# Layer 0's expert gather with eight fetch buffers in place of twelve

## The chip, the cores and the metric

The kernel runs on one core of a Trainium2 chip. The metric is the time of one execution on the device in microseconds (us). Two runs of the kernel before took 4397.53 and 4405.12 us, median 4401.32.

## The reference

The reference computes two layers of a diffusion backbone over 512 latent and 256 context tokens of width 1024, in f32. Layer 0 mixes tokens by a Fourier transform and a bidirectional state-space scan, layer 1 by latent attention. After each mixer comes the same channel mixer, PEER, which is what this change touches:

```python
q = (hb @ p["peer_wq"]).reshape(PEER_TOKEN_BLOCK, PEER_HEADS, 2, PEER_QDIM // 2)
s = jnp.einsum("thsd,hskd->thsk", q, p["peer_keys"]).astype(jnp.float32)
s_top, i_top = lax.top_k(s, PEER_TOPK)
...
u = jnp.take(p["peer_u"], experts, axis=0)
act = jax.nn.gelu(jnp.einsum("thkd,td->thk", u, hb)...) * gates
v = jnp.take(p["peer_v"], experts, axis=0)
return jnp.einsum("thk,thkd->td", act.astype(v.dtype), v)
```

Each token picks 16 of 16384 experts in each of 8 heads. An expert is a row u and a row v of 1024 numbers. The token's dot product with u, through a gelu and times a gate, is the weight with which v is added to the token's output. Layer 0 does this for all 768 tokens, layer 1 for the 512 latent ones.

## The kernel before

The whole core memory is one tensor, the arena, and all places in it are given by hand as offsets. `peer_block` runs the channel mixer for a layer. It works on tiles of 128 tokens, one token on each partition, six tiles in layer 0 and four in layer 1. A *step* is one head of one tile (48 in layer 0). A step has 16 *gathers*: gather k fetches, for each of the 128 tokens, the row pair (u, v) of its k-th expert, 2048 f32 numbers a token, 1 MB in all, into one buffer. Four gathers make a *position* (`BATCH`), so layer 0 has 192 positions and 768 gathers. Both rows of an expert stand side by side in HBM, so one indirect DMA fetches both.

The order of work is written out by hand, engine by engine, with semaphores between the engines:

- GpSimd (lines 1663 to 1680) only issues the gathers. Before each step it waits for the step's expert numbers, and before each gather it waits until the buffer's earlier gather has been used (semaphore `free`). The buffer of a gather comes from `slot_of` (line 1447): the gathers go round the buffers of the map in order.
- VectorE (`dot_batch`, line 2198) waits for each landing and computes the dot product of u with the token's row, line 2206. After the dots of a position it does other work in a fixed order: `choose_a` or `choose_b`, the two halves of a later step's choice of experts (line `half_at`, 1421: one half per position, until all 48 steps are chosen, at position 92), and the gated identity for the next two positions (line 2194).
- ScalarE (`diagonals`, line 2036) applies the gelu (line 2040) and writes four scaled diagonal matrices (line 2046).
- TensorE multiplies each diagonal with v and adds into the tile's output (line 1876), eight products for a position; the second product of each gather raises `free`. Between positions TensorE also computes queries (line 1764) and scores for later choices (`query_at`, one event for up to four tiles), and, from position 130 on, the down projection of layer 1's attention for finished tiles (`prepare`, line 1800).
- At the change of a tile VectorE gates the tile's output and adds it to x (`add_tile`, lines 2212 and 2214), and TensorE's first products of the next tile wait for that.
- The queue of SyncE loads query weights and keys for the coming events, then the weights of the down projection, and at the end of the gather the query and key weights of the attention (lines 1654 to 1661). The last two go where the first fetch buffers lie, so they wait until buffers 0 to 2, and 0 to 4, have been used for the last time.

Layer 1 has its own map with twelve buffers, of which the first 16 gathers use only eight; it is not changed. The core of GpSimd's loop is

```python
if uses:
    pool.wait_ge(free["sem"], at(free, prev + 1))
...
pool.indirect_dma_start(slots[n], None, tbl,
                        bass.IndirectOffsetOnAxis(ap=expert[:, ring[c], k:k + 1], axis=0)
                        ).then_inc(land[n]["sem"], up(land[n], 16))
```

Of the kernel before, what the change touches and what calls it, by code (L numbers as in the profile page):

```python
# [53 lines left out]
RO = XO + TT * D  # L54
SLOT = 4096
HO = RO + 3 * SLOT
L0 = HO + KD * TOK
# [1169 lines left out]
def attention_stage(core, d):  # L1227
# [30 lines left out]
    with nc.Block() as block:  # L1258
# [94 lines left out]
ROWS = 2 * D  # L1353
# [10 lines left out]
               [(7, (2, 3, 4, 5)), (0, (1,)), (0, (2, 3, 4, 5)), (1, (1,))] +  # L1364
               [(h, (2, 3, 4, 5)) for h in range(1, PH - 1)],
     "heads": (ALL, ALL[2:] + ALL[:2]) + (ALL[7:] + ALL[:7],) * 4, "kept": (), "order": None, "w": RO,
     "choose_from": 1, "spread_at": (1, 2), "small": 12, "ring_from": 0,
     "g1": L0 + 15360, "g2": L0 + 17408,
     "diag": L0 + 18432, "wq": L0 + 19968, "sc": L0 + 22016, "keys": L0 + 24064,
     "rep": (L0 + 3072, L0 + 5120), "ht": HO,  # L1370
     "slots": [RO + n * ROWS for n in range(6)] + [L0] + [L0 + 7168 + n * ROWS for n in range(5)]},
    {"events": [(h, (0,)) for h in range(4)] + [(h, (0, 1, 2, 3)) for h in range(4, PH)] +
               [(h, (1, 2, 3)) for h in range(4)],
     "heads": (ALL,) + (ALL[4:] + ALL[:4],) * 3, "kept": (4, 5, 6, 7),
# [1076 lines left out]
```

## Time and profile before

| | |
|---|---|
| median of two runs | 4401.32 us |
| profiled execution | 4394.9 us from first to last instruction (its span) |
| layer 0's gather | from 721.7 us (first issue) to 2707.1 us (last dot) |
| busy in the whole span | TensorE 3112.4 us (71%), VectorE 2859.6 (65%), GpSimd 1584.1 (36%), ScalarE 1122.0 (26%) |
| software DMA queue (the gathers) | 1342.26 MB, 73.8% of sixteen engines' span |
| mean granted clock of TensorE | 0.843 |

Times in the profile count from the first instruction. PE is TensorE, DVE is VectorE, ACT is ScalarE, POOL is GpSimd, SP is SyncE. A row of a timeline gives the start, the duration, the engine, the line, the operation, how many are merged into the row, and in brackets how long the engine sat idle before it and what ended that. "DMA to landing" is the time from the start of the issue to the last of the sixteen engines' signals.

### The profile page before, as it was taken

What the parts mean: (1) busy time and instruction counts of PE and PEld (TensorE: products, weight loads), DVE (VectorE), ACT (ScalarE), POOL (GpSimd) and SP (SyncE); (2) the same over time, 40 slices, a digit from 0 to 9 for tenths busy, and PEclk for the clock granted to TensorE, in tenths of its full rate; (3) what the DMA queues carried; (4) which work ended last, traced back from release to release, by engine and by line L of the source; (5) the groups of instructions that cost most, each with busy time, mean ns of one, the idle gap of its engine ahead of it and who ended that gap; (6) DMA issues with size and microseconds to landing.
All of it is one profiled execution on the core that took longest, in us unless ns stands there. A gap on an engine that the chain in (4) does not pass through costs nothing. (4 is left out here: it accounts for less than half of the span.)

```text
span 4394.9 us, 37634 instructions
## 1 busy us (share of the span) xinstructions
PE 3112.4 (71%) x12112; PEld 1324.7 (30%) x12112; DVE 2859.6 (65%) x7084; ACT 1122.0 (26%) x2966; POOL 1584.1 (36%) x1383
## 2 busy tenths in 40 slices
PE   7999987676666865656666656999876755555555
PEld 4655554332222321111222112565432311111111
DVE  2524853988888897555555555665788898555554
ACT  1122531322232322111222211563332222111111
POOL 0002401545444454444444441001344455444443
PEclk9999998888887887777787887999987877777777
DMA  4114734999999999999999996103999999999998
GB/s 172 39 39 146 264 105 170 408 420 421 420 420 409 402 421 420 421 421 417 412 415 421 415 421 286 39 1 116 403 420 420 419 421 417 418 420 418 418 420 340
DMA packets 223656, 1471.78 MB, mean 335 GB/s; under 512 B 25436, under 2 KB 29244, under 8 KB 53220
## 3 DMA queue, kind: packets, MB, share of 16 engines
q0 software_dynamic: 184320, 1342.26, 73.8%
q1 hardware_dynamic: 37764, 123.17, 7.8%
q10 hardware_dynamic: 1376, 3.96, 0.2%
q8 instruction: 96, 1.57, 0.1%
q14 instruction: 100, 0.82, 0.0%
HBM read 1467.02 MB, written 2.28 MB: 334 GB/s over the span
## 5 line engine op out<-in xcount | busy, mean ns | idle before, releaser
L1876 PE MATMUL banks<-arena 128*64 128x512 f32 x5120 | 1672.8, 814 | 1215.1 <-ACT arena L2046 1172.1
L1678 POOL DMA_INDIRECT arena<-experts,arena x1280 | 1507.7, 1178 | 2300.9 <-PE banks L1876 1478.7
L2206 DVE CUSTOM_DVE_ANT_0 arena<-arena 128x1024 f32<-128x1024 f32 x1280 | 1535.0, 1224 | 788.7 <-DMA arena<-experts,arena 788.5
L1876 PEld LDWEIGHTS banks<-arena 128*64 128x64 f32 x5120 | 458.4, 185 | 2356.0 <-ACT arena L2046 1364.7
L2040 ACT ACTIVATE arena<-arena 128x4 f32<-128x4 f32 x320 | 66.1, 206 | 2339.7 <-DVE arena L2206 2339.6
L2046 ACT ACTIVATE arena<-arena 128x64 f32<-128x64 f32 x1280 | 340.6, 336 | 36.3
L1764 PE MATMUL banks<-arena 128*128 128x512 f32 (+3 forms) x960 | 288.5, 455 | 6.0 <-DMA arena<-wq 5.4
L434 PE MATMUL banks<-arena 128*128 128x512 f32 (+1 forms) x640 | 208.6, 486 | 1.9 <-PEq L201 1.9
L1764 PEld LDWEIGHTS banks<-arena 128*128 128x128 f32 x960 | 160.6, 191 | 112.0 <-issue 86.6
L870 POOL TENSOR_TENSOR arena<-arena 128x256 f32<-128x256 f32 x48 | 41.2, 858 | 423.6 <-POOLq L625 332.3
L1697 PE MATMUL banks<-arena 128*128 128x512 f32 x416 | 185.4, 599 | 2.3 <-PEq L953 1.5
L434 PEld LDWEIGHTS banks<-arena 128*128 128x128 f32 x640 | 120.6, 190 | 86.2 <-issue 78.6
L2040 ACT ACT_TABLE_LOAD x90 | 115.5, 1283 | 1.6
L2194 DVE TENSOR_TENSOR arena<-arena 128x512 f32<-128x512 f32 x160 | 109.5, 685 | 0.0
L2206 DVE DVE_READ_ACCUMULATOR2_ANT arena<- 128x1 f32 x1280 | 105.9, 83 | 0.0
L1697 PEld LDWEIGHTS banks<-arena 128*128 128x128 f32 x416 | 77.6, 192 | 92.5 <-issue 92.4
L1962 ACT ACT_TABLE_LOAD x80 | 102.6, 1283 | 1.4
L1308 DVE TENSOR_REDUCE arena<-banks 128x1 f32<-128x768 f32 x64 | 61.2, 956 | 58.8 <-PE banks L1271 56.6
L1271 PE MATMUL banks<-arena 96*128 96x512 f32 (+1 forms) x256 | 96.5, 501 | 1.9 <-PEq L1600 1.5
L455 PE MATMUL banks<-arena 128*128 128x512 f32 x192 | 83.2, 593 | 0.0
L777 ACT ACTIVATE arena<-banks,arena 128x128 f32<-128x128 f32 x192 | 54.8, 368 | 105.9 <-PE banks L888 105.8
L1096 PE MATMUL banks<-arena 128*128 128x512 f32 (+1 forms) x192 | 75.4, 540 | 0.0
(250 smaller groups left out, 2942.7 us busy)
## 6 DMA issues: line engine op xcount, KB each, us to landing
arena<-l_w_ada SPq DMA_DIRECT2D x48, 1024.0 KB, 5.0
arena<-wq SPq DMA_DIRECT2D x54, 512.0 KB, 7.9
arena<-experts,arena POOLq DMA_INDIRECT x1280, 17.1
arena<-l_w_in SPq DMA_DIRECT2D x7, 2048.0 KB, 7.9
arena<-l_w_out SPq DMA_DIRECT2D x4, 1536.0 KB, 8.8
arena<-l_w_o SPq DMA_DIRECT2D x4, 1024.0 KB, 10.0
arena<-keys SPq DMA_DIRECT2D x27, 128.0 KB, 10.4
arena<-gates SPq DMA_DIRECT2D x6, 512.0 KB, 6.5
```

The costliest lines, as they stand in the source:

```text
L434: i = pe.matmul(o[:, a:b], wt[:, k, (u % 4) * P:(u % 4 + 1) * P], ht[:, k, a:b], start=(k == 0), stop=(k == KD - 1))
L455: i = pe.matmul(core["ps"][:, n % 4, :], ht[:, k, t * P:(t + 1) * P], wt[:, k, :], start=(k == 0), stop=(k == KD - 1))
L1271: i = pe.matmul(o[:, a:b], qt[0:QK, h, q * P:(q + 1) * P], kt[0:QK, h, a:b], start=True, stop=True)
L1678: pool.indirect_dma_start(slots[n], None, tbl, bass.IndirectOffsetOnAxis(ap=expert[:, ring[c], k:k + 1], axis=0)).then_inc(land[n]["sem"], ...
L1697: i = pe.matmul(core["ps"][:, bank_of(c), :], lhs(k, t), wcols[c][:, k, :], start=(k == 0), stop=(k == K - 1))
L1764: i = pe.matmul(core["ps"][:, 2 + side, 0:len(g) * P], wq[:, side, k, :], ht[:, k, g[0] * P:(g[-1] + 1) * P], start=(k == 0), stop=(k == K ...
L1876: mm = pe.matmul(core["ps"][QS * j:QS * j + QS, c, :], diag[:, g % 2, k, :], v[:, D + c * 512:D + (c + 1) * 512], start=(g % (NB * PH) == ...
L1962: act.activation(raised, shifted, ACT.Exp, accum_out=total[:, 0:1]).then_inc(exd["sem"], up(exd))
L2040: act.activation(gel[:, s], dots[:, s], ACT.Gelu).then_inc(gl["sem"], up(gl))
L2046: ins = act.activation(diag[:, g % 2, j, :], gated[:, b // 2, b % 2 * BATCH + j, :], ACT.Copy, scale=gel[:, b * BATCH + j:b * BATCH + j + 1])
L2194: dve.tensor_tensor(gated[:, n % 2], ident2.unsqueeze(1).to_broadcast([P, TOPK // 2, QS]), bcast(gate[:, ring[c], n % 2 * 8:n % 2 * 8 + 8] ...
L2206: dve.tensor_tensor_reduce(u, u, rep[i // PH % 2][:, k % NQ, :], 1.0, 0.0, ALU.mult, ALU.add, dots[:, k:k + 1]).then_inc(dot["sem"], up(dot))
```

## The change

Layer 0's map gets eight buffers. `small` goes from 12 to 8, and the list of places keeps its first eight entries; the last four are gone. Everything else follows from the length of that list: `slot_of`, the semaphores for the landings, and the gather that each wait names.

```diff
-     "choose_from": 1, "spread_at": (1, 2), "small": 12, "ring_from": 0,
+     "choose_from": 1, "spread_at": (1, 2), "small": 8, "ring_from": 0,
...
-     "slots": [RO + n * ROWS for n in range(6)] + [L0] + [L0 + 7168 + n * ROWS for n in range(5)]},
+     "slots": [RO + n * ROWS for n in range(6)] + [L0, L0 + 7168]},
```

The four places that fall out are used by nothing else.

## Rows read from the trace of the kernel before

**Rows 1.** The page: what the DMA moved, in 40 slices of the span.

```profile
GB/s 172 39 39 146 264 105 170 408 420 421 420 420 409 402 421 420 421 421 417 412 415 421 415 421 286 39 1 116 403 420 420 419 421 417 418 420 418 418 420 340
```

**Rows 2.** Busy windows: length, PE, PEld, DVE, ACT, POOL, clock, DMA share, GB/s.

```profile
761.00:1708.00 947.00, 636.46 (x2624) 250.10 (x2624) 841.10 (x2517) 274.24 (x697) 468.25 (x364) 0.83 1.01 415
1708.00:2708.00 1000.00, 600.95 (x1942) 187.50 (x1942) 545.25 (x930) 183.37 (x605) 426.41 (x389) 0.78 1.00 415
```

**Rows 3.** Waits: line 2206 in 761 to 1708, all in 1708 to 2708.

```profile
  DMA arena<-experts,arena: 29.4, 32
...
DVE arena L2206 <- DMA arena<-experts,arena: 421.5, 353, 2.3
```

**Rows 4.** Timeline of VectorE's dots, second half.

```profile
1797.04 1.23 DVE L2206 CUSTOM_DVE_ANT_0 arena<-arena 128x1024 f32<-128x1024 f32 x1 [1.25 <-DMA arena<-experts,arena]
1806.98 1.23 DVE L2206 CUSTOM_DVE_ANT_0 arena<-arena 128x1024 f32<-128x1024 f32 x1 [1.25 <-DMA arena<-experts,arena]
1819.41 1.23 DVE L2206 CUSTOM_DVE_ANT_0 arena<-arena 128x1024 f32<-128x1024 f32 x1 [0.64 <-DMA arena<-experts,arena]
```

**Rows 5.** Timeline of TensorE and GpSimd in the same stretch.

```profile
1809.69 5.79 PE L1876 MATMUL banks<-arena 128*64 128x512 f32 x16 [4.60 <-ACT arena L2046]
1813.64 0.94 POOL L1678 DMA_INDIRECT arena<-experts,arena  x1 [4.62 <-PE banks L1876]
```

**Rows 6.** Timeline of last dots and of one gather issue, first half.

```profile
1144.46 1.22 DVE L2206 CUSTOM_DVE_ANT_0 arena<-arena 128x1024 f32<-128x1024 f32 x1
1153.44 1.23 DVE L2206 CUSTOM_DVE_ANT_0 arena<-arena 128x1024 f32<-128x1024 f32 x1
1164.36 1.22 DVE L2206 CUSTOM_DVE_ANT_0 arena<-arena 128x1024 f32<-128x1024 f32 x1
1174.28 1.23 DVE L2206 CUSTOM_DVE_ANT_0 arena<-arena 128x1024 f32<-128x1024 f32 x1 [0.95 <-DMA arena<-experts,arena]
1151.11 1.98 POOL L1678 DMA_INDIRECT arena<-experts,arena  x1 [4.51 <-PE banks L1876]
```

**Rows 7.** Landings: second half; issues at 721.7; 768.8; 3051.4 (eight); 3099.5.

```profile
DMA to landing us min/median/max: 11.7/17.3/26.6
...
DMA to landing us min/median/max: 6.4/6.4/6.4
...
DMA to landing us min/median/max: 6.6/6.6/6.6
...
L1678 POOL DMA_INDIRECT arena<-experts,arena x8: 934/940/1651, 3051.4 to 3061.0; - x8
...
DMA to landing us min/median/max: 5.5/11.5/17.8
...
DMA to landing us min/median/max: 5.7/5.7/5.7
```

**Rows 8.** Timeline of a wide query event, TensorE and GpSimd.

```profile
1173.76 7.03 PE L1764 MATMUL banks<-arena 128*128 128x512 f32 x16
1180.72 3.65 PE L1876 MATMUL banks<-arena 128*64 128x512 f32 x16
1183.43 1.51 POOL L1678 DMA_INDIRECT arena<-experts,arena  x1 [5.87 <-PE banks L1876]
```

**Rows 9.** Timeline of a down projection, VectorE, TensorE and GpSimd.

```profile
2256.05 1.23 DVE L2206 CUSTOM_DVE_ANT_0 arena<-arena 128x1024 f32<-128x1024 f32 x1 [1.25 <-DMA arena<-experts,arena]
2255.13 9.31 PE L1800 MATMUL banks<-arena 128*128 128x512 f32 x32
2266.57 1.85 POOL L1678 DMA_INDIRECT arena<-experts,arena  x1 [8.48 <-PE banks L1876]
```

**Rows 10.** Waits, second half; SP's last load; its landing by the DMA view.

```profile
PE banks L1876 <- DVE arena L2214: 15.6, 3, 5.8
...
2707.57 0.49 SPq L1660 DMA_DIRECT2D arena<-l_w_ukv  x1
...
arena<-l_w_ukv SPq DMA_DIRECT2D x1, 2048.0 KB, 14.1
```

## The prediction

> **What bounds the kernel now.** I read the page's 40 slices first, then the busy windows of layer 0's gather, then who waits for whom in it, and last single positions in time. The gather runs from slice 7 to slice 24, and from slice 7 to 23 the DMA moves 402 to 421 GB/s [rows 1]. The two windows of it say the same: the DMA share is full in both, while VectorE is busy 841 of 947 us in the first and 545 of 1000 us in the second [rows 2]. The kernel has 192 positions of four gathers in this layer; half a choice of experts follows the dots of each of the first 93, which is what fills VectorE until 1708 us. So the second half is bound by the DMA alone: VectorE idles before its dots until a fetch lands, 421.5 us in 353 pieces [rows 3]. In the first half that wait is 29.4 us [rows 3], because VectorE and the DMA need nearly the same time: the last dots of three successive positions start at 1144.46, 1153.44 and 1164.36, intervals of 8.98 and 10.92, together 19.90 [rows 6]. The DMA's own pace, from two last dots that both waited for a landing, is 1806.98 - 1797.04 = 9.94 per position, 2.49 per gather [rows 4], so 19.9 for two positions. Both resources are full there, so a hole in the stream of transfers isn't filled again later.
>
> **What the change removes.** No instruction goes and none is added: 768 gathers, their dots, diagonals and products stay. GpSimd's wait before a gather now names the product that read the buffer eight gathers ago instead of twelve, so a position's fetch waits for the position two before it, not three. GpSimd does nothing else in the gather, so only fetches are queued behind that wait. With twelve buffers, the time from the release to the need was three positions less the processing; with eight it is two. That is the whole sum: does one turn of a buffer fit into two positions, 19.9 us?
>
> **The turn, second half.** Let T be the start of a position's last dot. At T = 1806.98 gelu and diagonals follow, the products start at 1809.69, and the first gather that reuses a freed buffer is issued at 1813.64, T + 6.66 [rows 4, 5]. Under the change this issue fetches for the position two later, whose first dot starts at 1819.41 [rows 4] and can't be later without a loss, since the DMA feeds it without pause. It has 1819.41 - 1813.64 = 5.77 us to land. How long does a fetch take that has little queued ahead? The median of 17.3 us [rows 7] is 6.9 gathers' worth of pace, mostly queueing, and says nothing here. The nearest rows are fetches that found the DMA empty or nearly so: 6.4, 6.6, 5.5 and 5.7 us [rows 7]; the mean is 6.05, and I take 6.1. The first of them had cold queues and the second still had two fetches ahead of it, so 5.5 is the lower end and 6.6 the upper. At 6.1 the turn is 6.66 + 6.1 + 3 x 2.49 = 20.2, 0.3 over two positions. Both positions of a pair are late by the same amount at once, so I charge a pair once: 0.3, plus 0.1 as an estimate for the step starts, where GpSimd takes one more wait first. 1708 to 2708 us holds 50 pairs: 50 x 0.4 = **20 us** (ends: 0 at 5.5; 50 x 0.9 = 45 at 6.6).
>
> **The turn, first half.** At T = 1144.46 the issue is at 1151.11, T + 6.65 [rows 6]. Here the position two later finishes its dots at 1164.36, and its first fetch must have landed 7.46 before, at 1156.90: 5.8 us to land, the same as above. But VectorE's intervals alternate, 8.98 and 10.92, and the DMA needs 9.94 for each; that fits only if the even position is in place about 1.0 ahead of its last dot, and this lead must now come out of the turn. With P for two positions, the lead is P less the turn L, and the rest has to hold 9.94 + 10.92, so P = (9.94 + 10.92 + L) / 2. With L = 6.65 + 6.1 + 7.46 = 20.2, P = 20.53, 0.63 more than 19.90. 46 pairs lie between 761 and 1708: **29 us** (ends: L = 19.6 gives 0.33, so 15; L = 20.7 gives 0.88, so 40).
>
> **Disturbances that twelve buffers absorb.** A third position in flight covers a late release; two don't. Eight wide query events fall into the first half. In one of them TensorE runs a query of 7.03 us from 1173.76, the position's products start only at 1180.72, and the issue is at 1183.43, which is 9.15 after that position's T of 1174.28, 2.5 more than the usual 6.65 [rows 6, 8]. 8 x 2.5 = **20 us** (ends: 16, where part lands beside the DMA's own load of the weights; 40, if each event's two positions both cost). Five times in the second half the down projection of the next layer's preparation takes TensorE 9.31 us; at T = 2256.05 the issue comes at 2266.57, T + 10.5, 3.9 over the usual [rows 9]. 5 x 3.9 = **20 us** (ends 10 and 30). At five changes of tile TensorE waits for VectorE's add; three such waits of the second half come to 15.6 us with one of 5.8 in it [rows 10]. The longest, less the 4.60 that TensorE idles before its products in any position [rows 5], is 1.2, so I take one microsecond each: **5 us** (0 to 10).
>
> **Start and end.** The first pass issues eight fetches at once instead of twelve; the four others were needed only after VectorE's work of the start. I take 0; if that cover is missing it costs at most one position's transfer, 10 us. At the end the load of the key weights waits for buffer 4, which is now last used in the last position rather than the one before, some six microseconds later. Before, it was issued at 2707.57 behind the query weights and took 14.1 us to land [rows 10]; issued later it finds those gone, so its landing stays, cost 0 (at most 3). Layer 1 has its own ring and doesn't change.
>
> Sum: 20 + 29 + 20 + 20 + 5 = 94 us. The profiled execution took 4394.9 us, 6.4 below the median of 4401.3; I put the sum on the median: **4495 us**. The lower ends sum to 41 (4442), the upper ones to 165 and 13 for start and end (4579).
>
> On the latency a page of the Trainium skill speaks, "DMA: Bandwidth & Descriptors", section "Anatomy of one DMA — SWDGE (gpsimd) path": a GpSimd-issued DMA takes about 2.0 us plus its bytes at 436 GB/s, which for the 1 MB of a gather gives an estimate of 4.4 us. The trace's shortest landing here is 5.5 us [rows 7], so it doesn't agree at either end. By that rule the turn would be 18.5 and both turn terms would vanish.
>
> **Rivals.** *Two positions cover the turn (not slower).* A fetch behind one or two others lands as soon as the one ahead of it plus 2.49, and the bare latency stays at or under 5.5 us; then the turn is 19.6, under 19.9, and only part of the disturbances is left: 41 us or less, around 4440, within 2%. The place is the first fetch of each position, the price up to 53 us less than forecast, and it decides where the landing takes less than 5.8 us. For it: the landings of 5.5 and 5.7 [rows 7], and the 6.6 may have been queueing only. Against it: the cold 6.4, and disturbances that have no slack left even at 5.5. That page's rule is this rival's mechanism. Chance 0.28, with the cases in between.
>
> *The latency grows in the stream (much slower).* The queue runs nearly dry each time, and the slowest of the sixteen engines ends the landing, say 7.8 us after the issue instead of 6.1. Then the second half's turn is 21.9, 2.0 over (100 us), and the first half's L of 21.9 exceeds the formula's P, so it costs 2.0 x 46 = 92; with the 45 of disturbances and some overlap of the two, 4401 + 237 = about 4640. For it: in the burst of eight issued from 3051.4 to 3061.0 the longest landing was 17.8 us [rows 7], where 5.5 and seven transfers of 2.49, less the 9.6 between first and last issue, give 13.3; other loads may be in that. Against it: the stream holds 2.49 exactly where it is fed [rows 4]. Chance 0.18.
>
> *The change doesn't do what it says.* The list of places and the small ring both have eight entries, so the ring has eight; a gain could come only from weights queueing behind fewer fetches, and VectorE and DMA would stay full. Chance 0.02, 4395.
>
> The forecast has 0.52. The range goes to 4438 below, where the pure disturbance case begins, and to 4610 above, past the upper ends and part way to the third case. About 2% (88 us) is what a measurement of this kernel tells from no change; that line, 4489, runs just below my forecast. Of the span from 4442 to 4579, 0.66 lies above it, so slower has 0.52 x 0.66 + 0.18 = 0.52, within 2% 0.46, and faster keeps the 0.02 of the last rival.
>
> **What would show it.** GpSimd's issue to landing falls from 17.3 us to about 7 to 9. The second half grows from 1000 to about 1043 us, DVE's wait for landings grows by as much, and the DMA's rate falls from 415 to about 400 GB/s. In the first half DVE's wait for landings, 29.4 us, rises above 60. If the rate stays at 415, the turn fits and I am too high; if single last dots stand more than 10.6 apart all through the second half, the latency is over 7 and I am too low. A change in layer 1 or in the attention would contradict the whole account.

## The result and the profile after

The changed kernel takes 4599.11 us (two runs, 4597.70 and 4600.52) where the kernel before takes 4401.32 us: 1.0449 times as long, with a 95% interval of 1.0433 to 1.0466. I had forecast 4495 us, so the direction was right, and the size, 198 us, is twice the 94 us of my sum. The profiled execution has a span of 4598.5 us against 4394.9.

The page's row of the DMA's rate in 40 slices answers to [rows 1]:

```profile
GB/s 165 55 21 185 267 38 242 380 384 375 389 382 366 388 372 384 380 381 378 389 370 367 379 382 378 140 37 22 273 418 419 421 416 418 421 421 419 419 421 340
```

From slice 7 to slice 24 the gather of layer 0 now gets 366 to 389 GB/s where it had 402 to 421; it is some 9% slower everywhere in this layer, in both halves. From slice 29 to slice 38, in layer 1, which has its own ring, the rate is back at 416 to 421. So the loss is a slower flow, not a few stalls.

Busy windows of the changed kernel, with the columns of [rows 2]: the 947 us of the first half, and the second half from its start to the last dot.

```profile
761.00:1708.00 947.00, 620.52 (x2464) 243.24 (x2464) 771.02 (x2291) 251.69 (x641) 417.87 (x330) 0.79 0.95 376
1799.00:2905.00 1106.00, 619.49 (x1942) 191.60 (x1942) 547.41 (x929) 183.48 (x605) 429.96 (x392) 0.75 0.96 378
```

The second half holds nearly the same work as the second window of [rows 2] (VectorE 547 against 545 us) and takes 1106 us instead of 1000. The DMA share fell only from 1.00 to 0.96 while the rate fell by 9%: so the share understates a starved stream, and the GB/s column is the one to read. The granted clock of TensorE fell too, from 0.78 to 0.75 in the second half and from 0.83 to 0.79 in the first. It has no part in the loss: the release, into which TensorE's products go, comes as soon after the dots as before (below).

Who waited for landings in those two windows, answering to [rows 3]:

```profile
  DMA arena<-experts,arena: 105.4, 94
```

```profile
  DMA arena<-experts,arena: 528.8, 370
```

29.4 us became 105.4 in the first window, which now ends some nine positions short of the work that it held before (up to 1799 us, where the first half now ends, it is 112.9), and 421.5 became 528.8 in the second, 107.3 more. The last dots of the positions, counted from 0, give the same division: from the one of position 1 to the one of position 92 the gather took 946.0 us before and 1038.2 now, +92.2; from there to the end 999.4 and 1106.1, +106.7. Together that is 199 of the 203.6 us by which the span grew. Five more lie behind the gather: 0.4 between its last dot and layer 1's first gather, 4.4 in layer 1's gather (1329.8 before, 1334.2 now). The 4.4 don't belong to the change: the two kernels below with twelve places and a wait of eight, which lose the same in layer 0, have 1329.9 and 1328.7 there.

Where in a position is the time lost? The timeline of some of VectorE's dots in a quiet stretch of the second half (compare [rows 4]; the last dots of four positions start at 1932.09, 1941.99, 1953.45 and 1963.96):

```profile
1932.09 1.22 DVE L2206 CUSTOM_DVE_ANT_0 arena<-arena 128x1024 f32<-128x1024 f32 x1 [1.25 <-DMA arena<-experts,arena]
...
1941.99 1.23 DVE L2206 CUSTOM_DVE_ANT_0 arena<-arena 128x1024 f32<-128x1024 f32 x1 [1.21 <-DMA arena<-experts,arena]
...
1944.48 1.22 DVE L2206 CUSTOM_DVE_ANT_0 arena<-arena 128x1024 f32<-128x1024 f32 x1 [0.62 <-DMA arena<-experts,arena]
...
1948.48 1.23 DVE L2206 CUSTOM_DVE_ANT_0 arena<-arena 128x1024 f32<-128x1024 f32 x1 [2.77 <-DMA arena<-experts,arena]
...
1950.98 1.23 DVE L2206 CUSTOM_DVE_ANT_0 arena<-arena 128x1024 f32<-128x1024 f32 x1 [1.26 <-DMA arena<-experts,arena]
...
1953.45 1.23 DVE L2206 CUSTOM_DVE_ANT_0 arena<-arena 128x1024 f32<-128x1024 f32 x1 [1.23 <-DMA arena<-experts,arena]
...
1956.24 1.23 DVE L2206 CUSTOM_DVE_ANT_0 arena<-arena 128x1024 f32<-128x1024 f32 x1 [1.56 <-DMA arena<-experts,arena]
...
1963.96 1.23 DVE L2206 CUSTOM_DVE_ANT_0 arena<-arena 128x1024 f32<-128x1024 f32 x1 [1.45 <-DMA arena<-experts,arena]
...
1968.81 1.23 DVE L2206 CUSTOM_DVE_ANT_0 arena<-arena 128x1024 f32<-128x1024 f32 x1 [3.01 <-DMA arena<-experts,arena]
```

And GpSimd's first issues of three positions in the same stretch, answering to [rows 5]:

```profile
1938.74 0.94 POOL L1678 DMA_INDIRECT arena<-experts,arena  x1 [7.09 <-PE banks L1876]
...
1948.64 1.88 POOL L1678 DMA_INDIRECT arena<-experts,arena  x1 [4.57 <-PE banks L1876]
...
1960.62 0.94 POOL L1678 DMA_INDIRECT arena<-experts,arena  x1 [6.35 <-PE banks L1876]
```

T = 1932.09 gives an issue at 1938.74, T + 6.65, and 1941.99 gives 1948.64, T + 6.65: the release is the one of the kernel before (the third, 1960.62, comes at T + 7.17). What it fetches is wanted by the first dots at 1944.48, 1956.24 and 1968.81. These dots start 5.74, 7.60 and 8.19 us after the issues. Where one is as short as 5.74, the dot is on time but the next one comes 4.00 us later instead of 2.49 (1944.48 to 1948.48). The last dots stand 9.90, 11.46 and 10.51 us apart. The time from an issue to the last dot of its position is what counts, and in no position of this gather is it below the 13.6 us that I had (6.1 and three times 2.49; the shortest is 13.76): 1938.74 to 1953.45 is 14.71, 1948.64 to 1963.96 is 15.32.

Over positions 94 to 129, a quiet stretch, it is 15.31 us in the median and 15.48 in the mean, of which 7.80 and 7.87 to the first dot. 6.65 + 15.48 = 22.1 is the turn; two positions take 22.1 us there, before 20.0. That the two agree is no proof: from a last dot to the issue, and from there to the last dot two positions on, is the same path measured in two pieces. What the pieces tell is which of them grew. The first half has the same turn with VectorE's work around it (compare [rows 6]):

```profile
1164.33 1.23 DVE L2206 CUSTOM_DVE_ANT_0 arena<-arena 128x1024 f32<-128x1024 f32 x1 [0.54 <-DMA arena<-experts,arena]
...
1174.24 1.23 DVE L2206 CUSTOM_DVE_ANT_0 arena<-arena 128x1024 f32<-128x1024 f32 x1 [0.94 <-DMA arena<-experts,arena]
...
1186.01 1.23 DVE L2206 CUSTOM_DVE_ANT_0 arena<-arena 128x1024 f32<-128x1024 f32 x1 [0.77 <-DMA arena<-experts,arena]
```

```profile
1170.98 1.98 POOL L1678 DMA_INDIRECT arena<-experts,arena  x1 [7.53 <-PE banks L1876]
```

1164.33 + 6.65 = 1170.98, and from there 15.03 to 1186.01: two positions in 21.68 us, 1.8 more than the 19.90 of [rows 6].

Last, the SyncE queue's load of the key weights, to be held against [rows 10]:

```profile
arena<-l_w_ukv SPq DMA_DIRECT2D x1, 2048.0 KB, 9.0
```

It is issued 6.4 us after the last dot and lands in 9.0 us instead of 14.1, and layer 1's first gather comes 344.7 us after the last dot, before 344.3.

### The profile page after: what moved, and what is told of

Same layout as the page of the kernel before. It is cut to its first block and busy times, and to the rows that moved or that the text cites. A ratio compares the mean times of both kernels' runs of the same rounds, so it can differ in the third digit from the quotient of the medians.

```text
span 4598.5 us, 37630 instructions
## 1 busy us (share of the span) xinstructions
PE 3163.0 (69%) x12112; PEld 1335.0 (29%) x12112; DVE 2869.1 (62%) x7084; ACT 1121.3 (24%) x2966; POOL 1584.0 (34%) x1383
## 5 line engine op out<-in xcount | busy, mean ns | idle before, releaser
L1876 PE MATMUL banks<-arena 128*64 128x512 f32 x5120 | 1723.4, 835 | 1364.0 <-ACT arena L2046 1300.3
L1876 PEld LDWEIGHTS banks<-arena 128*64 128x64 f32 x5120 | 469.6, 190 | 2542.4 <-ACT arena L2046 1490.7
```

What stands on the lines that cost most here:

```text
L1876: mm = pe.matmul(core["ps"][QS * j:QS * j + QS, c, :], diag[:, g % 2, k, :], v[:, D + c * 512:D + (c + 1) * 512], start=(g % (NB * PH) == ...
```

## The experiments

My theory after the result: the turn of a buffer is what bounds layer 0 now, and the landing of a position's first fetch costs not 6.1 us but about 7.9 while the stream runs. Its rivals: the places (what lies beside the dropped buffers, or the load of the weights), many small disturbances in place of a steady loss, and a DMA that is slower with fewer fetches in flight at all times.

**Same twelve places, wait of eight.** Only the number in GpSimd's wait changes; the ring keeps its twelve buffers.

```diff
-                        pool.wait_ge(free["sem"], at(free, prev + 1))
+                        held = u - 8 if layer == 0 else prev
+                        pool.wait_ge(free["sem"], at(free, held + 1))
```

> Twelve buffers stay in their places, but in layer 0 GpSimd waits before each gather for the product that used the gather eight before, as the changed kernel does. Theory (the turn: release, issue, landing and three more transfers must fit into two positions, 19.9 us, and don't): the same loss as the change, 4590 to 4610 us, with pairs of positions of about 22.2 us in the second half. Rival (the places of the buffers or the number of semaphores cost): 4401 or well below 4590.

Measured: 4594.92 us against 4398.0, ratio 1.0453 [1.0435, 1.0470], the same as the change. The halves grew to 1036.4 and 1102.1 us. So places, landing semaphores and the end of the gather play no part; it is the wait alone. In this kernel the trace gives the landings from 1850 to 2700 us, to set against the 11.7, 17.3 and 26.6 of [rows 7]:

```profile
DMA to landing us min/median/max: 5.4/9.0/16.1
```

**Wait of eight for the first fetch of a position only.** The three others keep their wait of twelve.

```diff
+                        held = u - 8 if layer == 0 and u % BATCH == 0 else prev
```

> Twelve buffers, and only the first gather of each position waits for the gather eight before; the other three wait for the one twelve before, as in the kernel before. Theory (the first fetch of a position is the one that is late, the others follow it in GpSimd's order): 4570 to 4610 us, nearly the whole loss. Rival (the later three fetches are late too, by the second pair of products): clearly less, 4450 to 4550 us.

Measured: 4598.16 us, ratio 1.0460 [1.0442, 1.0477], halves 1029.8 and 1106.5. The three other waits cost nothing of their own: GpSimd issues in order, and the three follow the first at the same median distances of 1.24, 1.40 and 1.25 us in both kernels. The whole price hangs on one fetch in four.

**Eight buffers for the first half only.** The ring is small until gather 368 and has twelve buffers from there.

```diff
-     "choose_from": 1, "spread_at": (1, 2), "small": 12, "ring_from": 0,
+     "choose_from": 1, "spread_at": (1, 2), "small": 8, "ring_from": 368,
```

> Twelve buffers, but the first 368 gathers (92 positions) go round eight of them, the rest round all twelve. Theory (the turn is too long in both halves): only the first half loses, about 90 of the 198 us, so 4485 to 4500 us. Rival (the loss comes from wide query events and VectorE's work alone): nearly all 198 us, above 4560. Rival (it is lost only where the DMA alone is the bound): under 4430.

Measured: 4482.08 us, ratio 1.0189 [1.0172, 1.0206]. First half 1043.2 us, second 997.7, so the loss is in each half by itself and the two add up. The time is 3 us under the 4485 that I expected. The execution behind the halves is the slowest of the four (4493.14), so they show some 11 us more than the median does: by medians the first half's loss is 84 us of the 198. The windows show the step in the DMA's rate (last column), here for 761 to 1708 us and 1799 to 2800 us:

```profile
761.00:1708.00 947.00, 614.24 (x2448) 241.52 (x2448) 764.26 (x2263) 249.70 (x636) 423.27 (x328) 0.80 0.95 373
1799.00:2800.00 1001.00, 604.47 (x1948) 188.29 (x1946) 549.39 (x943) 183.32 (x605) 436.89 (x392) 0.78 1.01 420
```

**Nine and ten buffers.** One or two of the four dropped places come back.

```diff
-     "choose_from": 1, "spread_at": (1, 2), "small": 8, "ring_from": 0,
+     "choose_from": 1, "spread_at": (1, 2), "small": 9, "ring_from": 0,
...
-     "slots": [RO + n * ROWS for n in range(6)] + [L0, L0 + 7168]},
+     "slots": [RO + n * ROWS for n in range(6)] + [L0] + [L0 + 7168 + n * ROWS for n in range(2)]},
```

> Nine buffers in layer 0. The first fetch of a position then waits for the last gather of three positions ago and only the second waits for the release that the first waited for with eight; it has 2.49 us more, 8.3 us to land. Theory (a threshold: landings of about 7.9 us fit into 8.3): most of the loss is gone, 4405 to 4450 us. Rival (each buffer is worth the same, 198 us over four): about 4550 us.

> Ten buffers in layer 0. The release of a position's first products now feeds the third fetch of the position two later, with 10.8 us to land. Theory (threshold near 8 us, then only disturbances): 4400 to 4425 us, under the 4439 of nine buffers by what the disturbances cost there. Rival (linear in the number): 4495 us.

Measured: nine buffers 4439.23 us, ratio 1.0093 [1.0076, 1.0110], halves 967.2 and 1008.0; ten buffers 4409.59 us, 1.0025 [1.0013, 1.0038], halves 953.3 and 1001.8. One buffer gives back 160 of the 198 us. The ninth lets the first fetch of a position go a group earlier, and it is now the second fetch that waits for the late release. The timeline with nine buffers, GpSimd's first issue of a group and VectorE's dots:

```profile
1866.78 0.94 POOL L1678 DMA_INDIRECT arena<-experts,arena  x1 [5.85 <-PE banks L1876]
...
1876.71 0.94 POOL L1678 DMA_INDIRECT arena<-experts,arena  x1 [4.61 <-PE banks L1876]
```

```profile
1872.55 1.22 DVE L2206 CUSTOM_DVE_ANT_0 arena<-arena 128x1024 f32<-128x1024 f32 x1 [1.26 <-DMA arena<-experts,arena]
1875.03 1.23 DVE L2206 CUSTOM_DVE_ANT_0 arena<-arena 128x1024 f32<-128x1024 f32 x1 [1.25 <-DMA arena<-experts,arena]
1877.51 1.23 DVE L2206 CUSTOM_DVE_ANT_0 arena<-arena 128x1024 f32<-128x1024 f32 x1 [1.25 <-DMA arena<-experts,arena]
...
1884.97 1.23 DVE L2206 CUSTOM_DVE_ANT_0 arena<-arena 128x1024 f32<-128x1024 f32 x1 [1.27 <-DMA arena<-experts,arena]
```

The fetch issued at 1866.78 is used at 1875.03, the one issued at 1876.71 at 1884.97: 8.25 and 8.26 us, and in this stretch no dot stands more than 2.5 behind the one before it. So 8.25 us for the late fetch are enough for the full rate, two quiet positions take 20.0 us, and the threshold lies between this and the 5.77 us that eight buffers leave. What is left with nine, 41 us, isn't all the gather's: of the 42.4 us by which the profiled execution is longer, 21.2 lie in the first half, 8.6 in the second, 1.9 before the last dot of position 1 and 10.6 behind the gather, where no other kernel here loses more than 6 and no run says why.

**Eight buffers, each position worked in two halves.** In both layers ScalarE's gelu and diagonals follow after two dots each instead of four, and TensorE starts its first four products then (not shown), so the release comes earlier; the buffers stay eight.

```diff
+                for h in range(2):
+                    o = b * BATCH + h * NQ
+                    act.wait_ge(dot["sem"], at(dot, BATCH * g + (h + 1) * NQ))
+                    act.activation(gel[:, o:o + NQ], dots[:, o:o + NQ], ACT.Gelu).then_inc(gl["sem"], up(gl))
...
+                    ins.then_inc(dg["sem"], up(dg))
```

> Eight buffers as in the changed kernel, in both layers' code the position is worked in two halves: ScalarE takes gelu and two diagonals as soon as two dots are done and signals them, and TensorE starts its first four products then. That frees the first two buffers some 5 us earlier in the second half and 2.3 us earlier in the first. Theory (only the turn is too long): at least 11 and 9 us are left for a landing of about 7.9, so the loss is gone, 4395 to 4430 us with eight buffers. Rival (eight buffers hold too little for the DMA whatever the release): above 4540 us.

Measured: 4427.86 us, ratio 1.0061 [1.0045, 1.0078], halves 969.4 and 1012.7, two quiet positions 20.1 us. The release comes at T + 3.7 on average instead of T + 6.9 in the first half, and in the second, where the dots of a position stand further apart, at T + 1.2 instead of T + 6.7. That gives back 171 of the 198 us with the same eight buffers, so it isn't the number of buffers as such that slows the DMA, but the lateness of the release. The rival of too few fetches in flight isn't cut off by this: a fetch now spends 12.4 us between issue and dot instead of 9.5 (means of positions 94 to 129), so an earlier release also puts more of them in flight, and no run holds one of the two still. The windows of this kernel show the rate in the first and second half (last column):

```profile
761.00:1708.00 947.00, 628.48 (x2584) 238.18 (x2584) 823.85 (x2454) 295.11 (x772) 415.08 (x355) 0.83 0.99 403
1738.00:2746.00 1008.00, 599.18 (x1940) 163.88 (x1936) 543.03 (x919) 211.08 (x698) 430.82 (x392) 0.78 1.00 413
```

**Eight buffers, the diagonals signalled two and two.** The smallest shift: nothing else is reordered, TensorE starts its first products after two of four diagonals.

```diff
-                ins.then_inc(dg["sem"], up(dg))
+                    if j % NQ == NQ - 1:
+                        ins.then_inc(dg["sem"], up(dg))
```

> Eight buffers as in the changed kernel, but the diagonals are signalled two and two, so that TensorE starts and the first release comes about 0.48 us (two diagonals of 0.24) earlier. Theory (every microsecond of the turn counts once per two positions): 96 x 0.48 = 46 us less than the changed kernel, 4540 to 4570 us. Rival (the loss is a fixed cost of each restart of the DMA): within 15 us of 4597.

Measured: 4557.20 us, ratio 1.0369 [1.0351, 1.0386], inside the expectation. The release comes 0.48 us earlier (median T + 6.17) and the gather is 44 us shorter: 18.4 in the first half, 26.0 in the second, together 96 turns at 0.46. A release that is earlier by some time gives back nearly that time in each turn. These are single profiled executions; by the medians the gain is 40 us, with some 10 us of uncertainty, against 46 expected.

**Four more gelus, with eight and with twelve buffers.** The opposite shift: ScalarE does four idle gelus of the same four columns before the real one.

```diff
+                for again in range(4 if layer == 0 else 0):
+                    act.activation(spare[:, 4 * again:4 * again + 4], dots[:, s], ACT.Gelu)
```

> Eight buffers as in the changed kernel, and in layer 0 ScalarE computes four more gelus of four columns, into a spare place, before the one that counts, so that the release comes about 0.8 us later in every position. Theory (each microsecond of the turn counts once per two positions): about 96 x 0.8 = 77 us more than the changed kernel, 4650 to 4700 us. Rival (the loss is a fixed cost of the restart of the DMA): within 15 us of 4597.

> The same four extra gelus with the twelve buffers of the kernel before. Theory (with twelve, a release 0.8 us later is covered): 4395 to 4415 us. Rival (the extra work on ScalarE costs by itself): 4440 us or more.

Measured: with eight buffers 4619.32 us, ratio 1.0507 [1.0490, 1.0525], under my range of 4650 to 4700 and 7 us above the rival's 4612; with twelve 4400.56 us, 1.0008 [0.9999, 1.0018], no loss. I had added the durations of four gelus. The trace of ScalarE shows that they overlap:

```profile
1954.93 0.49 ACT L2042 ACTIVATE arena<-arena 128x4 f32<-128x4 f32 x4 [9.75 <-DVE arena L2209]
1955.33 0.19 ACT L2043 ACTIVATE arena<-arena 128x4 f32<-128x4 f32 x1
1955.63 1.06 ACT L2049 ACTIVATE arena<-arena 128x64 f32<-128x64 f32 x4
```

In the changed kernel, without them:

```profile
1954.72 0.21 ACT L2040 ACTIVATE arena<-arena 128x4 f32<-128x4 f32 x1 [10.07 <-DVE arena L2206]
1955.04 1.06 ACT L2046 ACTIVATE arena<-arena 128x64 f32<-128x64 f32 x4
```

The diagonals start 0.70 us after the first gelu instead of 0.32, so the delay is 0.38 us, and the median release moves from 6.65 to 7.03. 96 turns of 0.38 would be 36 us; measured were 20 to 22 (halves 1047.4 and 1118.5, 9.2 and 12.4 more). So a later release seems to cost 0.6 us for each microsecond, where the earlier one gave back 0.95 (0.46 of 0.48). That the two slopes differ isn't shown: by the medians, each held against the kernel before as it ran beside it, this kernel lost 24 us more than the changed one and the other gained 40, each with some 10 us of uncertainty, and both 36 and 46 lie at or inside these margins. The direction and the contrast with twelve buffers hold; the fixed cost is only weakly excluded by this run, and better by the two before it.

**Twelve buffers, wait of four.** Every position waits until the one before it is done, so its first fetch meets an empty DMA.

```diff
+                        held = u - 4 if layer == 0 else prev
+                        pool.wait_ge(free["sem"], at(free, held + 1))
+                    elif layer == 0 and u >= 4:
+                        pool.wait_ge(free["sem"], at(free, u - 3))
```

> Twelve buffers, but in layer 0 each gather waits for the product of the gather four before, so every position starts on a DMA that has run empty. It measures the disputed term, the landing of a first fetch. If a fetch on an empty DMA takes the 6.1 us that the prediction took, a position takes 6.66 + 6.1 + 7.46 = 20.2 us and the run is near 6320 us; then the rest of the 7.9 us in the changed kernel comes from the running stream. If every first fetch takes 7.9 us, a position takes 22.0 and the run is near 6670 us.

Measured: 6387.4 us (one run), near the number for a landing of 6.1. The issue and the next two dots in the second half:

```profile
3019.35 0.94 POOL L1681 DMA_INDIRECT arena<-experts,arena  x1 [15.96 <-PE banks L1879]
```

```profile
3024.95 1.23 DVE L2209 CUSTOM_DVE_ANT_0 arena<-arena 128x1024 f32<-128x1024 f32 x1 [10.21 <-DMA arena<-experts,arena]
3028.53 1.23 DVE L2209 CUSTOM_DVE_ANT_0 arena<-arena 128x1024 f32<-128x1024 f32 x1 [2.35 <-DMA arena<-experts,arena]
3031.03 1.23 DVE L2209 CUSTOM_DVE_ANT_0 arena<-arena 128x1024 f32<-128x1024 f32 x1 [1.27 <-DMA arena<-experts,arena]
3033.67 1.22 DVE L2209 CUSTOM_DVE_ANT_0 arena<-arena 128x1024 f32<-128x1024 f32 x1 [1.40 <-DMA arena<-experts,arena]
```

The first fetch is used 5.60 us after its issue, 5.64 in the mean, so my reading of [rows 7] was right for an empty DMA. But the second dot comes 3.58 later, not 2.49, and from the issue to the last dot it takes 14.32 us. That is one of the longer positions: over positions 94 to 129 the second dot comes 3.3 later in the median, and over the second half the whole takes 13.84. So even on an empty DMA the position was 0.3 longer than my 13.56, the first fetch shorter and the second longer; in the stream of the changed kernel it is 15.3.

**The version that beats both.** The halved positions with all twelve buffers; the edit is that of the halved positions above.

> The same work in two halves, with the twelve buffers of the kernel before. Theory (with twelve the turn has slack and the DMA is the bound): 4385 to 4405 us. Rival (the earlier release helps by itself, or the extra signals cost): more than 20 us away from 4398.

Measured: 4390.47 us, ratio 0.9984 [0.9974, 0.9993]: faster than the kernel before by 0.16%, some 7 us, and by 209 us than the changed one. The halves are as before, 945.6 and 999.5; the earlier release has nothing to give in a stream that is already full. Of the 7.7 us by which the profiled execution is shorter, 2.8 lie before the last dot of position 1 and 3.5 behind the last dot of layer 1, where the last position is finished sooner, and 1.5 between the two gathers.

## Why the prediction was right and wrong

- **The bound.** Right. Both halves were at the DMA's pace, and a hole in the stream wasn't filled later: +92.2 and +106.7 us, shown apart by the kernel with eight buffers in the first half only.
- **The release, T + 6.65.** Right: median 6.65 over positions 8 to 91, and 6.65 again in the rows above.
- **The landing of 6.1 us.** This is the step that failed. I took it from fetches that found the DMA empty or nearly so [rows 7], and that price is real there: 5.6 us in the kernel that waits for four. In the running stream the first dot came 7.80 us after the issue (median, positions 94 to 129), and the last one 7.6 behind it instead of 7.46 (means). So the second half's turn is 22.1, not 20.2: a pair costs 2.1 us, not 0.4, and 49.5 pairs make 105 of the 106.7 us, where my term was 20. In the first half the same path took 6.92 to the issue and 15.88 from there (means, positions 8 to 91), 22.8, above the P of my formula, so the turn itself sets the pair: two positions took 22.8 us, before 20.85, which makes 83 us on 42 pairs; my term was 29. Of the 92.2 us, the other nine come in the first eight positions.
- **What the 7.80 holds.** It is no bare latency. At the issue the position before still has fetches under way: its last dot comes 4.5 us later (median). Had each first dot stood at 5.6 us after its issue or 2.49 after the dot before it, whichever is later, it would have come 0.88 us sooner in the mean, and the second dot by the same rule 0.15. Twice their sum is 2.1 us, the whole loss of a pair. So with these two prices alone there would have been almost no loss, which is what my sum said; what it lacked is about 1 us in each position, which the stream loses when it is nearly dry. In the kernel that waits for four the same rule falls short by nothing at the first dot and by 0.72 us at the second, so most of that loss goes with every restart.
- **The rival of the latency that grows in the stream** is what happened. It named a landing of 7.8 us, 100 us for the second half and 92 for the first; measured were 7.80, 106.7 and 92.2. It gave 4640 as a total because it added 45 us of disturbances on top, of which the balance left little (below). I gave it 0.18 because I read the stream's pace of 2.49 as a sign of a short landing. It says nothing on that: three positions of 9.94 leave 15.7 us between release and need (29.8 less 6.65 and 7.46), and up to this the pace is kept whatever a landing takes.
- **The disturbances.** In the main mis-sized the other way, and the balance hides them. The second half has only 2 us beyond its quiet pairs (7 if the quiet stretch is ended one position sooner). But held against each kernel's own quiet pace, the five positions around each of the five down projections lose 9 us together in the changed kernel and none in the kernel before, where their release is as late (T + 9.5 to T + 10.6) and the pairs behind it stay at 19.8 to 21.0. So that term is real and half of my 20. Against it stands the load of the down projection's weights: in the six positions from 131 on the kernel before lost 8 us, with dots 3.4 apart, the changed one 5. With nine buffers the down projections cost 9 us too. In the first half the mean release is 0.27 us over 6.65, 11 us on 42 turns, where I had 20.
- **Tile changes, start, end.** The end cost 0.4 us, as I had it: a later issue, a shorter landing. The six positions around each of the three tile changes of the second half lost 2 us more than before, where I had 3; those of the first half weren't separated. The start I had at 0; of the nine us in the first eight positions no run tells how much is its own.
- **The rival of a turn that fits** fell. The Trainium skill, "DMA: Bandwidth & Descriptors", section "Anatomy of one DMA — SWDGE (gpsimd) path", has 2.0 us plus the bytes at 436 GB/s, an estimate of 4.4 us for the gather. The kernel that waits for four, with the DMA empty, measured 5.6; the shortest landing in the kernel with a wait of eight and twelve places is 5.4. The trace doesn't agree with it at any point here.
- **The signs I named.** DVE's wait rose above 60 (105.4). The median landing came to 9.0 us in the kernel with the same wait and twelve places, the upper end of 7 to 9. The rate fell below my 400, to 378. The last dots didn't stand over 10.6 apart all through: mostly they alternate, 9.9 and 11.4 to 13. Two turns run interleaved, the even and the odd positions', and only the sum of two intervals is set, 22. The mean, 11.2, is over that mark, so the sign should have been put on the pair. The second half grew to 1106, not 1043.

What makes a landing longer in the stream isn't settled, but the traces narrow it. A landing is complete when the last of sixteen engines has signalled. For the three first fetches shown above the signals come 5.07 to 5.72 us after the issue, 5.87 to 7.57, and 5.02 to 8.18; of the last one's, fifteen are in by 5.8 us, about as on an empty DMA (5.0 to 5.6), and the sixteenth comes 2.4 later. So there the landing is late by a single engine. More often several are late: over positions 94 to 129 the eighth signal of a first fetch comes after 6.2 us and the last after 7.8 (medians). The Trainium skill, "DMA: Bandwidth & Descriptors", section "Why a DMA increments its semaphore by 16 and not by 1", says that the engines of a transfer finish independently, and this trace agrees. The distance between the first and the last signal is 2.0 us with eight buffers (median, positions 94 to 129) and a steady 2.1 with nine, but 9.4 in the kernel before: there, of the fetch issued at 1943.36, fifteen signals come 6.4 to 9.4 us after the issue and the last at 16.1. So also in the full stream one engine is far behind the others, and the pace of 2.49 may be the pace of that one alone; this is argued, not shown. Which engine is late, and whether the rows it fetches or its queue make it so, no run here tells.

## What to carry to other kernels

With few buffers, work out the whole turn: release after the last use, landing of a fetch in the running stream, and the rest of the group at the DMA's pace; if it is longer than the time the other buffers cover, the difference is lost at every turn. Take the landing from a stream that has just been starved, or as what the full rate was seen to tolerate (here 8.25 us were enough and 6.25 were not), not from a fetch on an idle DMA (5.6 us). Read such a landing with what was still queued ahead of it. Before adding buffers, look at when the release comes: a release 3.2 us earlier in the first half and 5.5 in the second was worth 171 us here, a ninth buffer 160.

## What the runs showed of the hardware

- A 1 MB gather is used 5.6 us after its issue on an empty DMA, but the next one then comes 3.3 us behind (median) instead of 2.49. A stream whose first fetch of each position waits for a late release delivers 378 GB/s, one with the longer wait 415 to 421.
- Four more gelus of 128x4 ahead of one delay what follows by 0.38 us, about 0.10 each, while a single one is recorded with 0.21 us: they overlap, and a sum of their durations overstates the price. The Trainium skill, "ScalarE: Activation LUTs", states that activations back to back overlap by some 93 ns (section "What ACT_TABLE_LOAD costs"); this trace agrees (0.19 less 0.10), and my expectation had left it out.
- The DMA's busy share was 0.96 at 378 GB/s and 1.00 at 415.
- The sixteen signals of one gather lie 0.6 us apart when it is the first on an empty DMA (median), 2.0 in the starved stream, and 9.4 in the full stream of the kernel before, where one of them is some 7 us behind the fifteen others.
